# Compression of paged caches on TensorE: three products per pair of blocks instead of four, with first sums on POOL and second sums on VectorE

## The reference, cut to what matters

```python
CMP_BLK, CMP_STRIDE, CMP_HIDDEN = 32, 16, 256
def compress(rows, pos_emb, w1, w2):          # rows: 8 sequences x 1024 positions x 128
    idx = arange(n_cmp)[:, None] * CMP_STRIDE + arange(CMP_BLK)[None, :]   # n_cmp = 63
    blocks = rows[:, idx] + pos_emb
    hid = gelu(einsum('bnrd,rdh->bnh', blocks, w1))      # w1: 32 x 128 x 256
    return hid @ w2, idx[:, -1]
```

## Time and profile before

| what | value |
|---|---|
| median of 3 runs | 841.39 us |
| the profiled execution's own time | 842.18 us |
| its span | 840.4 us |
| TensorE (PE) busy | 765.9 us, 91% |
| VectorE (DVE) busy | 375.9 us, 45% |
| ScalarE (ACT) busy | 240.9 us, 29% |
| POOL busy, all of it DMA issue | 163.8 us, 19% |
| DMA | 213.27 MB, mean 254 GB/s |
| granted TensorE clock, mean | 0.956 |

### The profile page before, as it was taken

One profiled execution on the slowest core, in us unless ns is written; L12 is line 12 of the kernel. 1 busy time (PEld: TensorE's weight loads), 2 busy tenths in 40 slices (PEclk: granted clock), 3 DMA queues, 4 the chain that ended last, 5 costly groups with the idle time before them and its releaser, 6 DMA issues.

```text
span 840.4 us, 12834 instructions
## 1 busy us (share of the span) xinstructions
PE 765.9 (91%) x4940; PEld 418.4 (50%) x4940; DVE 375.9 (45%) x959; ACT 240.9 (29%) x601; POOL 163.8 (19%) x202
## 2 busy tenths in 40 slices
PE   6889999999997799998999998899899699999896
PEld 4455545544545344443554554545564355554553
DVE  3213688899876650106344233323655325321214
ACT  5324333222213201122154323334320133242222
POOL 0433312022230143350101022511132001001000
PEclk9989999999997799999999999999899899999799
DMA  8656768879884577688595394867679967857901
GB/s 291 211 191 225 258 258 306 311 259 414 313 289 150 190 251 273 237 294 318 183 333 178 141 397 168 289 249 286 241 243 387 372 223 289 301 174 277 331 1 53
DMA packets 67973, 213.27 MB, mean 254 GB/s; under 512 B 5072, under 2 KB 28928, under 8 KB 62024
## 3 DMA queue, kind: packets, MB, share of 16 engines
q0 software_dynamic: 20320, 142.55, 46.1%
q1 hardware_dynamic: 47432, 69.79, 23.7%
q10 hardware_dynamic: 160, 0.11, 0.0%
HBM read 206.39 MB, written 64.68 MB: 323 GB/s over the span
## 4 chain that ended last, share of the span: by engine, by line
PE 69%; DVE 14%; DMA 7%; issue 5%; ACT 4%; another core or an unknown queue 1%; DVEq 0%; ACTq 0%; SPq 0%
PE psum L957 28%; PE psum L1023 12%; PE psum L887 8%; PE psum L968 4%; DMA ring<-in_w_in_odd 4%; PE psum L1112 3%; PE psum L938 3%; PE psum L1078 2%; DMA ring<-in_cache_a_v,index_a 2%; PE psum L1376 2%; DVE SA L2442 2%; DVE ring L2439 1%; PE psum L1208 1%; PE psum L1297 1%
## 5 line engine op out<-in xcount | busy, mean ns | idle before, releaser
L957 PE MATMUL psum<-ring,XB 128*128 128x512 f32 (+3 forms) x760 | 331.4, 590 | 7.6 <-DMA ring<-in_w_in_odd 6.5
L957 PEld LDWEIGHTS psum<-ring,XB 128*128 128x128 f32 x760 | 144.9, 196 | 165.5 <-issue 154.9
L1023 PE MATMUL psum<-Z,ring 128*128 128x512 f32 x256 | 116.8, 600 | 1.4 <-issue 1.2
L1948 DVE TENSOR_TENSOR RT<-Z,const 128x128 f32<-128x128 f32 (+6 forms) x43 | 11.5, 267 | 148.7 <-ACT Z L1609 124.7
L1609 ACT ACTIVATE Z<-psum,stat 128x512 f32<-128x512 f32 (+3 forms) x38 | 24.1, 634 | 182.1 <-PE psum L957 168.6
L1023 PEld LDWEIGHTS psum<-Z,ring 128*128 128x128 f32 x256 | 46.5, 190 | 59.0 <-issue 58.0
L968 PE MATMUL psum<-ring,XB 128*8 128x128 f32 (+3 forms) x1664 | 50.4, 269 | 5.2 <-issue 3.7
L968 PEld LDWEIGHTS psum<-ring,XB 128*8 128x8 f32 x1664 | 41.7, 90 | 23.5 <-issue 22.5
L1519 ACT COPY NW<-psum 128x512 f32<-128x512 f32 (+1 forms) x56 | 32.7, 583 | 59.4 <-PE psum L887 58.4
L1773 ACT ACTIVATE SM<-SM,stat 128x128 f32<-128x128 f32 (+4 forms) x56 | 26.9, 480 | 65.1 <-DVE stat L2137 64.0
L887 PE MATMUL psum<-const,Z 128*128 128x128 f32 (+4 forms) x220 | 31.1, 275 | 7.3 <-DVEq L2561 3.9
(11 more groups left out here) (366 smaller groups left out, 907.9 us busy)
## 6 DMA issues: line engine op xcount, KB each, us to landing
ring<-in_w_in_odd SPq DMA_DIRECT2D x9, 2048.0 KB, 14.5
ring<-in_w_in_even SPq DMA_DIRECT2D x6, 2048.0 KB
ring<-in_cmp_w SPq DMA_DIRECT2D x4, 2048.0 KB
ring<-in_w_in_odd SPq DMA_DIRECT2D x8, 1024.0 KB
out_s_d_k<-in_state_d_k POOLq DMA_DIRECT2D x8, 1022.0 KB
out_s_d_v<-in_state_d_v POOLq DMA_DIRECT2D x8, 1022.0 KB
Z<-in_cmp_w POOLq DMA_DIRECT2D x5, 1024.0 KB, 8.1
ring<-in_state_d_v POOLq DMA_DIRECT2D x5, 1024.0 KB, 7.5
```

Source lines behind the costliest of these rows:

```text
L957: last = mm(out[:, 0:n], xT[:, k, t * 128:(t + 1) * 128], w[:, k * n:(k + 1) * n], start=k == 0, stop=k == KT - 1)
L1023: last = mm(out[:, h * 512:(h + 1) * 512], w[:, (r % 16) * CH + h * 128:(r % 16) * CH + h * 128 + 128], rowsT[:, at:at + 512], start=r == ...
```

## The change

For two neighbouring blocks 2m and 2m+1, with strips x: before, U x(2m) + L x(2m+1) and U x(2m+1) + L x(2m+2), four products. After: A = U (x(2m) + x(2m+1)), B = L (x(2m+1) + x(2m+2)), D = (L - U) x(2m+1); block 2m is A + D, block 2m+1 is B - D. Each product now runs over about 256 columns (A 257 with the bias column, B 249, D 256).

- `rowsT` has 32 planes of 260 columns, even strips in the first 16, odd ones in the others; ScalarE writes it with another pattern.
- The 16 positions of a strip go in 8 batches of 2 positions. For each batch POOL makes the first sums (128 x 514 elements into `pair_sums`, three buffers) and, when A of the batch is done, the weight differences (128 x 512, in place); VectorE makes the second sums (event `strips`, 128 x 496, in place). The 96 jobs for each kv (two matmuls' records each) are spread over the same 32 compress events, three for each; D comes two batches behind A.
- POOL's sums stand in its one queue among the gathers: what has a later place in ORDER than the event that frees a gather's slot is done behind that gather.
- The position-embedding columns are set by VectorE, the bias becomes two parts, and `hid_out` becomes one ScalarE copy of D's bank and four VectorE operations with 256 or 248 elements, which add or subtract D.
- D is summed in the second bank of the `scores` ring, so units of kind "b" claim both banks.
- The loads of w1 are two of 1 MB for each slot, sorted by batch; the first slot of w1 is released in step 21 instead of step 15.
- Two `select` rounds of gaps 28 and 30 and the one of the first `cache` event move behind; both first `a_values` move behind the last `cache` event.
- POOL's scratch for DMA descriptors is 8192 bytes of a partition instead of the default.

The diff, cut to its core. BATCHES is 8; `compress` is TensorE's, `strips` VectorE's, `weights_apart` and `first_sums` are POOL's.

```diff
+def compress_jobs():
+    jobs = []
+    for q in range(BATCHES + 2):
+        if q < BATCHES:
+            jobs += [(kind, q, j, h) for kind in "AB" for j in (0, 1) for h in (0, 1)]
+        if q >= 2:
+            jobs += [("D", q - 2, j, h) for j in (0, 1) for h in (0, 1)]
+    return jobs
+BATCH_AT = {JOBS.index(("A", q, 0, 0)) // 3: q for q in range(BATCHES)}
+def compress_steps(kv):
+    return [([("strips", kv, BATCH_AT[r] + 2)] if BATCH_AT.get(r, BATCHES) + 2 < BATCHES else [])
+            + [("compress", kv, r)] for r in BLK_ORDER]
...
-             27: [("output", 10), ("probs", 11), ("peak", "a")], 28: [("peaks", "a"), ("output", 11)] + select(),
-             29: [("shift", "a")] + select(), 30: [("exp_sum", "a")] + select(), 31: [("sums", "a")] + select()}
+             27: [("output", 10), ("probs", 11), ("peak", "a")], 28: [("peaks", "a"), ("output", 11)],
+             29: [("shift", "a")] + select(), 30: [("exp_sum", "a")], 31: [("sums", "a")] + select()}
...
-        order += ([("new_probs", "a")] if b == 2 else [("gelu", 0, 0)] if b == 5 else []) + select()
-        order += [values.pop(0)] if b in (6, 7) else []
-    order += [("gelu", 0, 1)]
+        order += ([("new_probs", "a")] if b == 2 else [("gelu", 0, 0)] if b == 5 else []) + (select() if b else [])
+    order += [("strips", 1, 0), ("strips", 1, 1), values.pop(0), values.pop(0), ("gelu", 0, 1)]
...
+                for kind, q, j, h in JOBS[3 * r:3 * r + 3]:
...
+                    if kind == "A":
+                        if begins:
+                            if q % 4 == 0:
+                                pe.wait_ge(*arrival[name])
+                            pe.wait_ge(sem("first_sums"), n)
+                        dst, rhs = out[:, h * 512:h * 512 + 257], pair_sums[:, q % 3, j, :]
+                    elif kind == "B":
+                        if begins:
+                            pe.wait_ge(sem("second_sums"), n)
+                        dst, rhs = out[:, h * 512 + 257:h * 512 + 506], rowsT[:, plane * PLANE + 8:plane * PLANE + 257]
+                    else:
+                        if begins:
+                            pe.wait_ge(sem("weights_apart"), n)
...
+            def strips(kv, q):
+                eng.wait_ge(sem("first_sums"), kv * BATCHES + q + 1)
+                x = even_strips(q, NB, 248)
+                tt(x, x, odd_strips(q, 248), add).then_inc(sem("second_sums"), 1)
+                wait_own(sem("second_sums"))
...
+            def weights_apart(kv, q):
+                w = slot_of(f"w1s{kv}_{q // 4}")
+                upper, lower = (w[:, at + 2 * q % 8 * CH:at + 2 * q % 8 * CH + 2 * CH] for at in (0, PART))
+                pool.wait_ge(sem("sums_used"), kv * BATCHES + q + 1)
+                nc.gpsimd.tensor_tensor(upper, lower, upper, ALU.subtract).then_inc(sem("weights_apart"), 1)
+            def first_sums(kv, q):
+                n = kv * BATCHES + q
+                if q == 0:
+                    pool.wait_ge(sem("bias_set"), kv + 1)
+                    pool.wait_ge(*marks["rows", kv])
+                if n >= 3:
+                    pool.wait_ge(sem("sums_used"), n - 2)
+                nc.gpsimd.tensor_tensor(pair_sums[:, q % 3, :, :], even_strips(q, 0, 257), odd_strips(q, 257), ALU.add)\
+                    .then_inc(sem("first_sums"), 1)
...
             for name, queue, parts in items:
                 if queue == "pool":
+                    freed = max([freed] + [last_use.get(n, others.get(n, len(ORDER)))
+                                           for n in place[name][1]])
...
+                    apart_until(freed)
                     stream(pool, name, parts)
```

More of the change, by code:

```diff
@@ L314, in even_order @@
         for j in (0, 1):
-            order.append(steps[2 * i + j])
+            order += steps[2 * i + j]
             if 6 <= i < 15 and j:
@@ L584, in build @@
         for kv in (0, 1):
-            for half in (1, 0):
-                src = ins["cmp_w1"][0, kv, half * 16:half * 16 + 16].rearrange("r d h -> d r h")
-                weights(f"w1s{kv}_{half}", [("full", src)])
+            for g in (0, 1):
+                src = [ins["cmp_w1"][0, kv, r:r + 8].rearrange("r d h -> d r h") for r in (8 * g, SUB + 8 * g)]
+                weights(f"w1s{kv}_{g}", [("full", src[0]), ("full", src[1], PART)])
         output_weights(0, (0, 1))
@@ L663, in build @@
                       before=["heads_read"], only=None),
-                 dict(slot="planes", view=Z[:, R0 + 6144:R0 + 6144 + PART], before=["w1s1_0"], only=None,
+                 dict(slot="planes", view=Z[:, R0 + 6144:R0 + 6144 + PART], before=["w1s1_1"], only=None,
                       span=(step_of["compress", 1, BLK_ORDER[-1]], step_of["rows", 1, 4, 0])),
@@ L683, in build @@
         late_last = [h["before"][0] for h in homes if h["slot"].startswith("late")]
+        turned_last = [h["before"][0] for h in homes if h["slot"] == "turned"]
         place["wout1_1"][1][:] = [h["before"][0] for h in homes if h["slot"].startswith("spare")]
@@ L1015, in compress @@
                     turned["out", kv] = P.filling
-                if r % 16 == 0:
-                    pe.wait_ge(*arrival[name])
-                if r == 0:
-                    pe.wait_ge(sem("tail_set"), due("pe", "tail_set"))
-                out, w = turned["out", kv], slot_of(name)
-                at = (r % 16) * PLANE + r // 16
-                for h in range(2):
-                    last = mm(out[:, h * 512:(h + 1) * 512],
-                              w[:, (r % 16) * CH + h * 128:(r % 16) * CH + h * 128 + 128],
-                              rowsT[:, at:at + 512], start=r == BLK_ORDER[0], stop=r == BLK_ORDER[-1])
@@ L1030, in compress @@
                 if r == BLK_ORDER[-1]:
-                    last.then_inc(P.full, 2)
+                    done.then_inc(P.full, 2)
                     release(name, P.full, P.made)
@@ L2704, in _ @@
                           peak=peak, peaks=peaks, shift=shift, exp_sum=exp_sum, sums=sums, new_probs=new_probs, a_values=a_values, a_norm=a_norm, mixed=mixed,
-                          out_rows=out_rows, mix=mix, gelu=gelu, second=second, fold=fold, hidden=hidden,
+                          pos=pos, strips=strips, hid_out=hid_out, out_rows=out_rows, mix=mix, gelu=gelu, second=second, fold=fold, hidden=hidden,
                           second_prompt=second_prompt, score_d=score_d, new_d=new_d, cmp_scores=cmp_scores, cmp_turn=cmp_turn,
@@ L2773, in _, with apart_until @@
             moves = list(MOVES)
+            def weights_apart(kv, q):
[12 more added lines that the diff above has]
+                    .then_inc(sem("first_sums"), 1)
+            apart = sorted([(step_of["compress", kv, JOBS.index(("A", q, 1, 1)) // 3], weights_apart, kv, q)
+                            for kv in (0, 1) for q in range(BATCHES)]
+                           + [(step_of["strips", kv, q], first_sums, kv, q) for kv in (0, 1) for q in range(BATCHES)],
+                           key=lambda x: x[0])
+            def apart_until(freed):
+                while apart and apart[0][0] < freed:
+                    _, work, kv, q = apart.pop(0)
+                    work(kv, q)
+            freed = -1
+            others = {"turn_x0": -1, "heads_read": step_of["scores", 11], f"win0_{LAST[0]}": step_of["decode_rows", 0, LAST[0]]}
             for name, queue, parts in items:
                 if queue == "pool":
+                    freed = max([freed] + [last_use.get(n, others.get(n, len(ORDER)))
+                                           for n in place[name][1]])
+                    freed = len(ORDER) if name == "w1p0_0" else freed
+                    apart_until(freed)
                     stream(pool, name, parts)
```

144 lines of the change are left out of this document (95 added, 49 removed).

## The result

The changed kernel takes **879.2 us** (median of 4, 875.8 to 883.8) against 840.7 for the kernel before (4 runs, 836.2 to 842.1): ratio **1.047**, interval 1.041 to 1.054. The forecast was 838.1 with a range of 825 to 850: wrong, and outside its range. The time was forecast to fall by 0.4% and rose by 4.7%.

The account below looks back on a forecast made before the run. TensorE was taken as the bound (766 of 840.4 us busy), with VectorE also full in kv 0. 5.2 + 0.2 - 9.2 + 0.5 = -3.3 us from 842.18 gave 838.9, less 0.8 for a median: 838.1, range 825 to 850.

Parts of the forecast that it names:

- TensorE, 13.7 us less for each kv: Compression matmuls: 384 shorter records at 0.215 us instead of 256 at 0.429, saving 27.4 us, 13.7 for each kv.
- VectorE waits for POOL, 10.8 us in kv 0: kv 0 compression: VectorE stands before strip sums until POOL's first sums, queued behind gathers, are done; 10.8 us together.
- Strip sums, 6 x 0.7 = 4.2: kv 0 compression: six second sums on VectorE at 0.7 us each with the gap, adding 4.2 us to its queue.
- Rival 2: kv 0: POOL's 14 operations and VectorE's two-input operations hold each other, VectorE's chain growing 7 + 2 us; 847 us, chance 0.26.
- POOL's operation, 1.0 us: POOL's first sums and differences: about 1.0 us each, taken from its gathers, with bounds of 0.7 and 2.3.
- Cache stage +0.2: Stage between the compressions: one search round fewer saves 1.8 us, `hid_out`'s four VectorE operations add 2.0; together +0.2.
- kv 1, -9.2: kv 1 compression: 30 steps save 12.9 us, less 1.7 and 1.5 for gathers and 0.5 for new waits; -9.2 us.
- The two terms for late gathers, 1.7 and 1.5: kv 1: first gathers issued later behind sums and moved `a_values`, +1.7 us; 18 loads sharing three slots, +1.5; each 0 to 5.
- Rival 3's clock: TensorE's idling in kv 0 lowers its granted clock, +4 to +5 us, or kv 1 gathers do; 843 us, chance 0.12 with rival 4.
- Smaller scratch, weights slot released later: Smaller DMA scratch: nothing, 2 us at most; w1 slot released in step 21, not 15: nothing, up to 6 us without cover.

Follow-up runs that it names:

- Run 5: Changed kernel with its three products only, POOL's sums and differences and VectorE's strip sums left out; kv 1 takes 90.5 us against 103.3 in the kernel before.
- run 9: Kernel before plus 32 unread POOL sums on a scratch row, a semaphore wait before each, and the smaller DMA scratch; loses some 4 us (0.5%).
- run 13: Changed kernel with POOL waiting on its own semaphore behind each first sum and each difference; not faster than the change, rather 1% slower.
- run 12: Kernel before, unchanged, profiled again on the same chip as runs 9 to 11; 824.6 us beside that group.
- Run 8: Changed kernel with each sequence's 32 columns side by side, so ScalarE's copies write contiguously; its profile has 4.3 us less than run 10, intervals overlap.
- run 11: Changed kernel with four products and no sums in kv 0, three products in kv 1 with sums and differences on VectorE, contiguous copies; ratio 0.997 to the kernel before.
- run 1: Kernel before with only ScalarE's copies of the transposed cache rows written at a step of 8 columns; 0.5% slower.
- run 2: Changed kernel with POOL's 16 weight differences left out, semaphore still raised; ratio 1.037 to the kernel before.
- run 4: Changed kernel with POOL's first sums placed early, up to three ahead, as soon as their buffer is free; ratio 1.034 to the kernel before.
- run 14: Run 4's kernel plus POOL waiting on its own semaphore behind each first sum and difference; ratio 1.027 to the kernel before.
- run 3: Changed kernel with VectorE's second (strip) sums and B's wait for them left out, POOL's work kept; 28 us come back by the ratios.
- run 7: Changed kernel with VectorE's strip sums of batches 0 and 1 in gap 12, not gap 5; layer 1 starts at 190.3 against 189.4 in run 10, no gain.
- run 10: Changed kernel run again unaltered, as the measure for the runs beside it; ratio 1.043 to the kernel before.
- run 6: Changed kernel with all sums and differences on VectorE, none on POOL, first two batches' sums in gap 12; ratio 1.022 to the kernel before.

## Why the prediction was wrong

The forecast had -3.3 us and the profiles have +35.6, 38.9 more: 15.2 of it in kv 1, 11.1 in kv 0, 11.0 in the start of layer 1, 3.7 in the cache stage, -2.1 in the rest. The step that failed most is kv 1's, which took VectorE's new work there as hidden and gave the new waits 0.5 us, where TensorE then stood 12.5 us behind VectorE; next are the strip sums of kv 0 at 0.7 us each. Step by step, by its own terms:

- **TensorE, 13.7 us less for each kv**: right for TensorE's own work. Run 5 has 12.8 less in kv 1, records at 0.216.
- **VectorE waits for POOL, 10.8 us in kv 0**: right in kind and size. Measured in front of the six strip sums: 2.0, 0, 3.2, 3.9, 2.1, 0, together 11.3 (forecast 1.7, 1.1, 2.8, 3.5, 1.7, 0). That the sum fits so well is partly luck: four waits were each 0.3 to 0.5 longer, mostly since POOL's sum took 1.3 and not 1.0, and the 1.1 of the second fell away because VectorE was still held.
- **Strip sums, 6 x 0.7 = 4.2**: this is where kv 0 failed. They took 4.17, 0.67, 1.65, 1.66, 2.87 and 0.68, together 11.7; two other operations of the chain were held for another 1.0 (the product at 263.52 and one at 261.55, 0.89 for 0.42). Product to product, from gap 16 to gap 26, VectorE's chain grew by 21.5 us, not 12, and TensorE needed 16.3 behind it instead of 14.5 (clock 0.88 against 1.00 before). With these kv 0 comes out at 83.1, where the step gave 72.
- **Rival 2** had the mechanism, with the wrong place, price and objection. It said "while VectorE waits for POOL there is nothing to collide with". But where another operation stands ready behind the sum, it is already under way when VectorE wakes: of the ten strip sums that waited for POOL seven met one and took 1.65 to 4.17 us, the other three took 0.67 to 0.68. The sign given for this rival, products over 2.3 or POOL's sums over 1.5 us, looked at the wrong operation; it was the strip sums that were held. At the 0.5 us for each of 14 operations it assumed it would give 7 us, close to the 7.5 seen in kv 0; that it came on top of the waits, not instead, and in kv 1 too, is what it missed. The rule of the Trainium skill ("SBUF — State Buffer", "SBUF: two separate sides"), "an exclusive lock, not a bandwidth split", is borne out in both directions: the strip sum at 214.90, POOL's first sum of 3.18 us beside a product in run 9. But the section has the engine that comes first keep the ports for one instruction, and at 214.90 VectorE was kept out for three of POOL's.
- **POOL's operation, 1.0 us**: 1.30 and 1.27 measured. Run 9's, with one row for inputs and result, takes 1.04. The gap isn't the reason: run 13 has it and 1.27 to 1.30 where VectorE isn't beside. What is, stays open. The estimate of 1.1 from the Trainium skill's figure ("GPSIMD Engine Reference", Elementwise — side-by-side cycle accounting) was nearer than 1.0, and low too.
- **Cache stage +0.2**: +3.9. The strided copies were costed at nothing "since the rows show no wait on SP's issue and POOL's gathers": no row about ScalarE was looked at. ScalarE is busy 19.2 of 33.1 us there, 11.6 of 27.8 in run 12, on the loop of transposes. Run 8 takes 2.3 of it back, run 11 nearly all. But the copies alone cost this stage 0.4 us (run 1). In the change `hid_out`'s copy stands behind six of them in ScalarE's queue, VectorE's part of `hid_out` waits for it, and TensorE's next count waits for VectorE:

```profile
285.49 6.66 ACT L1568 COPY Z<-psum 128x512 f32<-128x512 f32 x6 [7.31 <-PE psum L919]
```

```profile
293.06 0.18 DVE L2629 COPY Z<-posT 128x16 f32<-128x16 f32 x1 [2.36 <-ACT XB L1769]
```

```profile
295.37 0.56 PE L1302 MATMUL psum<-KC 128*128 128x7 f32 x2 [4.60 <-DVE PNT L2563]
```

  The step had VectorE's work in it and not this wait. The 2.36 us of it and 3.3 of work for the bias and `hid_out`, less the 1.8 of the round moved away, come to the +3.9.
- **Start of layer 1**: not treated. The same copies run in layer 0's first gaps: +4.5 in run 1, and 7.4 between runs 12 and 5, of which some 3 are the half clock near 49 us described under run 11. In its first profile the changed kernel has a further stretch, 101 to 109 us, in which TensorE stops several times for up to 1.1 us with nothing waited for ("issue"), and then runs at half clock; the profiles of runs 2, 4, 13 and 14 have it too, those of runs 1, 3, 7 and 10 don't. Its cause stays open. Sums moved into layer 0 bring it from 186.1 to 189.4 (runs 5 and 10).
- **kv 1, -9.2**: +6.0. The step gave POOL's sums +1.7 and the gathers +1.5 and took VectorE's work as hidden ("VectorE 27 of 102 us"). VectorE is busy for 41 us there now and waits another 13 in front of strip sums, and TensorE stands behind it: it is idle 20.7 us of this stretch where it was 7.1 before, and 12.5 of that, in three waits, is for VectorE's search, where before it had none. Its busy time falls by 7.4 us, not by 13, at a granted clock of 0.92. One such wait:

```profile
342.31 0.96 POOL L886 DMA_INDIRECT ring<-in_cache_b_k,index  x1 [4.18 <-PE psum L1425]
...
346.08 0.95 POOL L886 DMA_INDIRECT ring<-in_cache_b_k,index  x1 [0.30 <-issue]
347.05 1.28 POOL L2870 TENSOR_TENSOR pair_sums<-Z 128x514 f32<-128x514 f32 x1
```

```profile
348.44 0.68 DVE L2642 TENSOR_TENSOR Z<-Z 128x496 f32<-128x496 f32 x1 [5.09 <-POOL pair_sums L2870]
```

```profile
356.54 0.59 PE L1302 MATMUL psum<-KC 128*128 128x7 f32 x2 [7.89 <-DVE KC L2304]
```

POOL waits for a slot, issues four gathers of `cache_b_k` (342.31 to 347.03) and only then the first sum. VectorE stands 5.09 us in front of the strip sum, and the search behind it in VectorE's queue keeps TensorE idle for 7.89 us, where a turn of that loop cost 1.4. The written order, which the step used for kv 0, wasn't followed through kv 1. With all sums on VectorE kv 1 takes 97.7 (run 6), with nothing to wait for 90.5 (run 5). The two terms for late gathers, 1.7 and 1.5, did not come: TensorE waits 3.5 us for gathers here, 3.7 before. Run 9's profile has more of it, 6.0 us against 4.2.
- **Rival 3's clock** was a follower: with TensorE idling, the granted clock is 0.88 and 0.92 in the two compressions, where before it was 1.00 and 0.98 (run 12); in run 5, without the waits for sums, it is 0.97 and 1.00.
- **Smaller scratch, weights slot released later**: nothing seen, as forecast. The part behind layer 1's compression is 1.6 us shorter in the profile of the change, and 442.3 against 442.7 us in run 9, with the smaller scratch, against run 12. No run has the later release alone; no DMA is among what TensorE's compression matmuls wait for in the change.

What stays open: how the 35 us divide exactly. Against the change's 1.047 or 1.043, undoing one part at a time gives some 8 us (differences), 28 (second sums), 11 (early sums), 17 (all on VectorE), which overlap (those of the differences and the early sums are not clear of noise), since each wait covers another. Why run 11's tail gives back 5.9 us wasn't tried.

## What to carry to other kernels

Moving arithmetic to an idle engine isn't free when an engine with a full queue waits for its result, or when the two hold each other: here the same sums cost some 17 us less on VectorE, although that was already full in kv 0. Ask of each operation in a helper's queue what is issued ahead of it (four gathers) and what comes right behind it (a run of its own that keeps the woken engine out). And when a layout is changed, cost the engine that writes it, by a run or by a row of that engine, before costing what reads it.

## What the runs showed of the hardware

- A run of POOL operations with no gap (starts 1.23 us apart, each 1.29 long) kept a VectorE operation on two SBUF inputs out until the whole run was over: 4.17 us for 0.67, 7.11 for 2.29. With a semaphore wait and so 0.08 us between them VectorE got in after one at most in run 13. In run 14 a product of 4.26 us was kept out by a gather's issue, a copy's issue and a sum, which had no such wait between them.
- It goes both ways: the first of the six POOL sums in the row of 10.71 us of run 9 took 3.18 in place of 1.04 us beside a product, and the product 2.33. A gather's issue was held likewise, 2.58 us for 0.95 at 227.23 in run 3, beside a product from 226.70 to 228.99.
- ScalarE's copy of 128x512 from PSUM into SBUF takes 585 ns with 32 or 64 elements in a row, 1072 with a step of 8 elements on the written side.
